# First mixer: sums of squares against two columns of ones in place of 128

## The chip, the cores and the metric

The kernel runs on one core of a Trainium2 chip. The metric is the device time of one execution in microseconds (us); lower is better. The core has a matrix engine (TensorE, PE in the rows; its weight loads are listed apart as PEld), VectorE (DVE), ScalarE (ACT), GpSimd (POOL), and a queue that starts DMA transfers (SP). They run side by side and wait for each other by semaphores.

## The reference, cut to what matters

Two blocks of two layers each are computed for 256 tokens of width 1024, in float32. A layer of the first block is a mixer and then a mixture of experts. At its end the mixer normalises two halves of 512 features (attention heads, short convolution) apart and multiplies with `w_out`:

```python
def rmsnorm(x, g):
    y = x * lax.rsqrt(jnp.mean(x * x, axis=-1, keepdims=True) + EPS)
    return y * g

y_attn = windowed_gqa_with_sink(q, k, v, sink)            # (tokens, 512)
y_conv = gate_b * centred_short_conv(gate_c * u, conv_w)  # (tokens, 512)
y = jnp.concatenate([rmsnorm(y_attn, g_attn), rmsnorm(y_conv, g_conv)], axis=-1)
x = x + y @ w_out
```

So each token needs two sums of squares, each over 512 features: 4 numbers for each of 128 partitions, as the 256 tokens are two tiles of 128. The experts, the final norm and the whole second block follow and are not touched.

## The kernel before, in words

The kernel is one program of five instruction streams in an order written out by hand. `psum_tiles()` numbers every PSUM tile; tile n lies in bank n mod 8 and a semaphore for each bank counts fillings (`done`, `full`) and emptyings (`claim`, `emptied`). An engine executes its stream strictly as written, TensorE's included; its weight loads can run ahead of the matmuls in front of them.

In the first mixer everything before the norm is held with the features on the partitions: `yT` (the two halves, scaled by their gains) and `sq` (their squares, written by ScalarE at lines 812 and 831), each 8 blocks of 128 features by 256 tokens. A sum over features is a sum over partitions, which TensorE does: at line 1901, after the heads' loop, it takes a 128 by 128 block of `sq` (128 features, 128 tokens) as the stationary operand and the constant `ones` as the moving operand. The result has the tokens on the partitions, and every column of it holds the same sum. Four blocks of features are accumulated for each of the 2 halves and the 2 token tiles, so line 1901 has 16 matmuls in a layer. Each float32 matmul runs as two load-and-multiply pairs, so the trace shows 32 matmuls and 32 loads a layer, 64 of each in all. All four results lie in one PSUM bank, tile `("ss", layer, 0)`.

What reads it is one VectorE instruction at line 1249, which takes one column of each of the four results, and makes mean plus EPS. GpSimd raises that to the power -1/2 (line 683, `inverse_root`). VectorE then adds the products with `w_out` to `x`, scaled by these roots (line 1258, 8 times). The products are the tiles `out1`: `mixer_out(i)` at line 1858 makes each with 4 matmuls of 512 columns. Two of them (`out1` 0 and 1) stand ahead of the sums of squares on TensorE, beside the last heads, and six behind; after the fifth of those come transposes of `x` (line 1912), the router (line 1923, matmuls of 36 columns) and `keep_clock` (line 1739), matmuls of zeros with `ones` that have no result anyone reads.

In the expert stage (lines 1779 to 2063) line 2035 multiplies 128 by 128 blocks with a moving operand of 2 columns, 128 times in all.

Of the kernel before, what the change touches and what calls it, by code (L numbers as in the profile page):

```python
# [23 lines left out]
P = 128  # L24
# [166 lines left out]
def program(nc, x_in, cols_in, rows_in, rope1_in, gains_in, router_in, w_in, w_out, w_gate, w_up, w_down,  # L191
            positions, w_in2, w_lru, w_oa, w_or, w_o, out):
    with ExitStack() as ctx:
# [12 lines left out]
        ones = ctx.enter_context(nc.sbuf_tensor("ones", [P, P], F32))  # L206
# [15 lines left out]
        stat = ctx.enter_context(nc.sbuf_tensor("stat", [P, 64], F32))  # L222
# [11 lines left out]
        def carve(phase, *shape):  # L234
            n = int(np.prod(shape))
            at = top.get(phase, 0)
            top[phase] = at + n
            assert top[phase] <= WORK, (phase, top[phase])
            v = work[:, at:at + n]
            if len(shape) == 2:  # L240
                v = v.rearrange("p (a b) -> p a b", a=shape[0])
            if len(shape) == 3:
                v = v.rearrange("p (a b c) -> p a b c", a=shape[0], b=shape[1])
            return v
# [19 lines left out]
        sq = carve("mix1", KD, SEQ)  # L264
# [155 lines left out]
        def bank(name):  # L420
            return banks[TILE[name] % BANKS]
# [5 lines left out]
        def uses(name):  # L427
            return TILE[name] // BANKS + 1

        def full(eng, name):  # L430

            eng.wait_ge(psum_full[TILE[name] % BANKS], uses(name))
# [51 lines left out]
        def arrive2(eng, layer, j):  # L484

            at = layer * NB2 + j
            kind, _, n = B2_PIECES[j]
            eng.wait_ge(w_loaded["b2"][at % RING2], 16 * (at // RING2 + 1))
            if kind == "lru":
                return ring[:, at % RING2, 0:n].rearrange("p (b n) -> p b n", n=P)  # L490
            return piece(at % RING2, RT if kind == "or" else KD, n)
# [581 lines left out]
        def _(dve):  # L1073
            S = Steps(dve, own_dve)
# [92 lines left out]
            def first_mixer(layer):  # L1167
# [13 lines left out]
                for t in range(NT):  # L1181
                    a, b = heads[t][:, :, 0:ROT1], heads[t][:, :, ROT1:2 * ROT1]
# [5 lines left out]
                for t in range(NT):  # L1188
                    a, b = heads[t][:, :, 0:ROT1], heads[t][:, :, ROT1:2 * ROT1]
# [49 lines left out]
                for hh in range(HEADS):  # L1239
# [3 lines left out]
                    for nm, j in BESIDE_HEAD[hh]:  # L1243
                        if nm == "u":
                            gated_input(j)

                name = ("ss", layer, 0)
                full(dve, name)
                S.marks(dve.tensor_scalar(stat[:, 8:12], bank(name)[:].rearrange("p (a b) -> p a b", b=P)[:, :, 0],
                                          1.0 / CW, EPS, ALU.mult, ALU.add), psum_read[TILE[name] % BANKS], uses(name))  # L1250
                dve.wait_ge(rstd_ready, 5 * layer + 3)
                for i in range(8):
                    hf, t, part = OUT1[i]
                    name = ("out1", layer, i)
# [458 lines left out]
            for layer in range(DEPTH):  # L1713
                first_mixer(layer)
                last_hT(2 * layer + 1)
                router(layer)
                experts(layer)
# [7 lines left out]
        def _(pe):  # L1725
# [59 lines left out]
            for layer in range(DEPTH):  # L1785
# [12 lines left out]
                else:  # L1798
# [5 lines left out]
                    for k0 in (0, KD // 2):  # L1804
# [4 lines left out]
                        for t in range(NT):  # L1809
                            for k in range(k0, k0 + KD // 2):  # L1810
                                mm = pe.matmul(bank(("q", 0, t))[:], hT[:, k, t * P:(t + 1) * P], w[:, k],
                                               start=(k == 0), stop=(k == KD - 1))
# [16 lines left out]
                for j in range(3):  # L1829
                    name = ("qkT", layer, j)  # L1830
                    claim(name)
                    for k in range(2):
                        for t in range(NT):
                            src = (qkv[:, t, (2 * j + k) * P:(2 * j + k + 1) * P] if j < 2 else
                                   (qkv[:, t, QW:QW + KVW] if k == 0 else kswap[:, t]))
                            mm = pe.transpose(bank(name)[:, k * SEQ + t * P:k * SEQ + (t + 1) * P], src, ident[:])
# [27 lines left out]
                for hh in range(HEADS):  # L1864
                    if hh + 1 < HEADS:
                        scores(hh + 1)
                    name = ("PT1", layer, hh)
                    claim(name)
                    pe.wait_ge(probs, layer * HEADS + hh + 1)
                    for kb in range(NT):  # L1870
                        for qb in range(NT):
                            mm = pe.transpose(bank(name)[:, kb * SEQ + qb * P:kb * SEQ + (qb + 1) * P],
                                              s1[:, hh % 2, qb, kb * P:(kb + 1) * P], ident[:])
# [13 lines left out]
                    for kb in range(NT):  # L1887
                        mm = pe.matmul(bank(yn)[r, 0:SEQ], qkv[:, kb, v0:v0 + HD1], pT1[:, hh % 2, kb],
                                       start=(kb == 0), stop=(kb == NT - 1))
# [5 lines left out]
                name = ("ss", layer, 0)  # L1895
                claim(name)
                for part in range(2):
                    for t in range(NT):
                        o = (2 * part + t) * P
                        for j in range(4):  # L1900
                            mm = pe.matmul(bank(name)[:, o:o + P], sq[:, 4 * part + j, t * P:(t + 1) * P], ones[:],
                                           start=(j == 0), stop=(j == 3))
                done(mm, name)
                def turn_x(t):
# [31 lines left out]
                name = ("rank", layer, 0)  # L1936
# [7 lines left out]
                mm = pe.matmul(bank(name)[:, 2 * NE:3 * NE], ones[:], A[:, 1], start=False, stop=True)  # L1944
# [115 lines left out]
                for t in range(NT):  # L2060
                    for hf in range(2):
                        for part in (y_hi, y_lo):
                            mm = pe.matmul(banks[2 * t + hf][:], comb[:, 1, t * P:(t + 1) * P],
                                           part[:, hf * 512:(hf + 1) * 512], start=False, stop=True,
                                           skip_group_check=True)
# [3 lines left out]
            for layer in range(DEPTH):  # L2069
# [120 lines left out]
                for j in range(0, 12, 2):  # L2190
# [4 lines left out]
                    for k in range(cnt):  # L2195
                        for odd in range(2):
                            if j < 4:
                                hd, qb = 8 * (j // 2) + 2 * k + odd, 0
                            else:
                                hd, qb = 4 * ((j - 4) // 2) + 2 * k + odd, 1  # L2200
                            r = slice(64 * odd, 64 * odd + 64)
                            mm = pe.matmul(bank(names[odd])[:, k * w_:(k + 1) * w_], iqT[r, hd // 2, qb * P:(qb + 1) * P],
                                           ikT[r, 0:w_], start=True, stop=True)
# [8 lines left out]
                for j in range(RT):  # L2212
                    name = ("gates", layer, j)
                    claim(name)
                    mine = [(n, i) for n, (jj, i) in enumerate(BLOCK_PAIRS) if jj == j]
                    for g, wg_ in enumerate((wr, wi)):
                        for n, i in mine:
                            mm = pe.matmul(bank(name)[:, g * SEQ:(g + 1) * SEQ], wg_[:, n], xc[:, i],  # L2218
                                           start=(n == mine[0][0]), stop=(n == mine[-1][0]))
# [22 lines left out]
                for hh in range(HEADS):  # L2242
                    if hh + 1 < HEADS:
                        scores2(hh + 1)
                    name = ("PT2", layer, hh)
                    claim(name)
                    pe.wait_ge(probs2, layer * HEADS + hh + 1)
                    b = hh % 2
# [80 lines left out]
```

## Time and profile before

| | us |
|---|---|
| median of 3 runs | 1988.59 |
| lowest, highest | 1988.37, 1990.35 |
| profiled execution, its own time | 1990.61 |
| profiled execution, its span (first to last instruction) | 1988.9 |
| TensorE busy with matmuls | 1909.9 (96% of the span) |
| TensorE busy with weight loads | 1272.3 (64%) |
| VectorE busy | 734.3 (37%) |
| mean granted clock of TensorE | 0.992 of full speed |

A row of the trace gives the start in us from the span's start, the duration, the engine, the line of the kernel, the operation, what it writes and reads (`work` holds `sq`), the shape, and the number of instructions that were merged into the row. In brackets stands how long the engine was idle before and who ended that. The end of a matmul is modelled. "Granted clock" is the share of TensorE's full speed that the chip allowed; 1.00 is 2.4 GHz and 0.50 is 1.2 GHz.

### The profile page before, as it was taken

The numbers are of one execution on the slowest core, as the hardware profiler recorded it, in microseconds if no ns is written. First come the engines' busy times: TensorE is split into PE (matmuls) and PEld (weight loads), VectorE is DVE, ScalarE is ACT, GpSimd is POOL, SyncE is SP. The second block draws the span as 40 slices with busy tenths as digits, with TensorE's granted clock in tenths as the row PEclk, the third lists the DMA queues.
The fourth block names the chain that finished last, engine by engine and source line by source line (L and its number), as shares of the span: only waits on it lengthen the run. The fifth ranks groups of instructions, "written<-read, shape, count | busy, mean of one in ns | idle before, by whom it ended". The sixth has DMA issues, their size and how long they took to land.

```text
span 1988.9 us, 26083 instructions
## 1 busy us (share of the span) xinstructions
PE 1909.9 (96%) x10488; PEld 1272.3 (64%) x10488; DVE 734.3 (37%) x1679; ACT 606.5 (30%) x1170; POOL 266.5 (13%) x247
## 2 busy tenths in 40 slices
PE   8999999999998999999999999999999989999997
PEld 6764444444445754444444445887889968788996
DVE  3332111111112332111111114556665645656655
ACT  2311111111112321111111113556654534574654
POOL 1300000000000300000000003971000057710000
PEclk9999999999999999999999999999999999999999
DMA  9348999999998238999999996452425845433353
GB/s 363 113 169 363 427 428 427 428 429 428 428 417 302 87 147 366 428 427 427 428 428 428 429 428 231 138 199 85 167 81 160 287 143 170 167 122 110 111 177 118
DMA packets 121421, 557.47 MB, mean 280 GB/s; under 512 B 5008, under 2 KB 49584, under 8 KB 96240
## 3 DMA queue, kind: packets, MB, share of 16 engines
q1 hardware_dynamic: 119696, 551.51, 69.9%
q10 hardware_dynamic: 1440, 4.36, 0.6%
q8 instruction: 65, 1.06, 0.2%
q0 software_dynamic: 192, 0.30, 0.1%
q14 instruction: 28, 0.23, 0.0%
HBM read 555.11 MB, written 1.05 MB: 280 GB/s over the span
## 4 chain that ended last, share of the span: by engine, by line
PE 90%; ACT 4%; DVE 4%; issue 2%; POOL 0%; POOLq 0%; DVEq 0%
PE bank L2015 15%; PE bank L2046 11%; PE bank L2017 8%; PE bank L1771 7%; PE bank L1779 6%; PE bank L2160 3%; PE bank L2162 3%; PE bank L2161 3%; PE bank L1992 3%; PE bank L2139 3%; PE bank L2140 3%; PE bank L2141 3%; PE bank L1763 3%; PE bank L1858 3%; PE bank L2218 3%
## 5 line engine op out<-in xcount | busy, mean ns | idle before, releaser
L2015 PE MATMUL bank<-ring,work 128*64 128x512 f32 x512 | 224.9, 594 | 5.0 <-issue 5.0
L2017 PE MATMUL bank<-ring,work 128*64 128x512 f32 x512 | 224.9, 594 | 0.0
L727 POOL TENSOR_TENSOR w_lo<-ring,w_hi 128x512 fp32r<-128x512 f32 (+1 forms) x160 | 207.7, 1319 | 78.0 <-ACT w_hi L917 75.6
L683 POOL TENSOR_TENSOR stat<-stat,power 128x1 f32<-128x1 f32 (+1 forms) x18 | 10.8, 601 | 1502.2 <-DVE stat L1079 1465.4
L1421 DVE TENSOR_TENSOR work<-work,bank 64x512 f32<-64x512 f32 x64 | 43.9, 686 | 433.3 <-ACT work L872 433.3
L872 ACT ACTIVATE work<-bank 64x512 f32<-64x512 f32 x64 | 37.8, 591 | 474.3 <-PE bank L2017 474.3
L917 ACT CAST w_hi<-ring 128x512 fp32r<-128x512 f32 (+1 forms) x208 | 123.3, 606 | 131.4 <-PE bank L2162 87.7
L1640 DVE TENSOR_TENSOR w_lo<-ring,w_hi 128x512 fp32r<-128x512 f32 (+1 forms) x176 | 116.0, 678 | 79.3 <-ACT w_hi L1030 79.1
L1771 PE MATMUL bank<-hT,ring 128*128 128x256 f32 x640 | 143.6, 379 | 0.0
L1779 PEld LDWEIGHTS bank<-work,h 128*128 128x128 f32 x1024 | 116.7, 192 | 24.8 <-issue 24.8
L1030 ACT CAST w_hi<-ring 128x512 fp32r<-128x512 f32 (+1 forms) x176 | 104.0, 610 | 92.9 <-PE bank L2141 76.4
L1771 PEld LDWEIGHTS bank<-hT,ring 128*128 128x128 f32 x640 | 119.4, 190 | 15.7 <-issue 0.7
L1437 DVE SCALAR_TENSOR_TENSOR act_hi<-bank,stat,act_hi 128x512 fp32r<-128x512 f32 x64 | 48.1, 751 | 211.1 <-ACT act_hi L882 211.1
L2015 PEld LDWEIGHTS bank<-ring,work 128*64 128x64 f32 x512 | 68.5, 137 | 88.6 <-issue 86.6
L1779 PE MATMUL bank<-work,h 128*128 128x128 f32 x1024 | 122.8, 278 | 0.1
L2015 PE MATMUL bank<-ring_tail,work 128*64 128x512 f32 x256 | 113.0, 594 | 3.2 <-issue 3.2
L2046 PE MATMUL bank<-ring,work 128*64 128x512 f32 x512 | 113.4, 595 | 2.2 <-ACT work L877 0.8
L2015 PE MATMUL bank<-work 128*64 128x512 f32 x256 | 112.9, 594 | 2.5 <-issue 2.5
L2017 PE MATMUL bank<-ring_tail,work 128*64 128x512 f32 x256 | 113.1, 595 | 0.0
L2017 PE MATMUL bank<-work 128*64 128x512 f32 x256 | 113.0, 594 | 0.0
L882 ACT ACTIVATE act_hi<-bank,stat 128x512 fp32r<-128x512 f32 x64 | 44.0, 687 | 210.4 <-PE bank L2046 210.4
L753 ACT ACTIVATE work<-bank 128x256 f32<-128x256 f32 (+3 forms) x128 | 57.9, 476 | 154.9 <-PE bank L1771 61.1
(317 smaller groups left out, 3829.5 us busy)
## 6 DMA issues: line engine op xcount, KB each, us to landing
ring<-w_in_dram SPq DMA_DIRECT2D x34, 2048.0 KB, 9.1
ring<-w_gate_dram SPq DMA_DIRECT2D x32, 2048.0 KB, 18.5
ring<-w_up_dram SPq DMA_DIRECT2D x32, 2048.0 KB, 23.0
ring<-w_down_dram SPq DMA_DIRECT2D x32, 2048.0 KB, 23.2
ring_tail<-w_down_dram SPq DMA_DIRECT2D x16, 2048.0 KB, 21.0
work<-w_gate_dram SPq DMA_DIRECT2D x16, 2048.0 KB, 18.5
work<-w_up_dram SPq DMA_DIRECT2D x16, 2048.0 KB, 22.9
ring_tail<-w_gate_dram SPq DMA_DIRECT2D x16, 2048.0 KB, 19.9
```

The source lines that it names most:

```text
L727: pool.tensor_tensor(w_lo[:, g % CHUNKS, 0:n], w[:, k], w_hi[:, g % CHUNKS, 0:n], ALU.subtract).then_inc(chunk_lo, 1)
L917: act.copy(w_hi[:, g % CHUNKS, 0:w.shape[2]], w[:, k]).then_inc(chunk_hi, 1)
L1030: act.copy(w_hi[:, g % CHUNKS, 0:src.shape[1]], src).then_inc(chunk_hi, 1)
L1640: dve.tensor_tensor(w_lo[:, g % CHUNKS, 0:n], src, w_hi[:, g % CHUNKS, 0:n], ALU.subtract).then_inc(chunk_lo, 1)
L1763: mm = pe.matmul(bank(name)[:, 0:n], hT[:, k, t * P:(t + 1) * P], w[:, k, 0:n], start=(k == 0), stop=(k == KD - 1))
L1771: mm = pe.matmul(dst, w[:, k, f * P:(f + 1) * P], rhs[:, k], start=(k == 0), stop=(k == nk - 1))
L1779: mm = pe.matmul(dst[:, kk * P:(kk + 1) * P], h[:, t, k * P:(k + 1) * P], pick[:, b, t], start=(t == 0), stop=(t == NT - 1))
L1858: mm = pe.matmul(bank(name)[:], yT[:, 4 * part + j, t * P:(t + 1) * P], w_[:, 4 * part + j], start=(j == 0), stop=(j == 3))
L1992: mm = pe.matmul(banks[2 * t + hf][:], comb[:, p % 2, t * P:(t + 1) * P], part[:, hf * 512:(hf + 1) * 512], start=(first and p == 0 and pa ...
L2015: pe.matmul(m_bank(m)[gate, :], lhs, wg[:, k], start=(k == 0), stop=(k == KD - 1), skip_group_check=True)
L2017: mu = pe.matmul(m_bank(m)[up, :], lhs, wu[:, k], start=(k == 0), stop=(k == KD - 1), skip_group_check=True)
L2046: mm = pe.matmul(m_bank(m0 + T_OUT + hf)[r, :], hidT[:, f * P + 64 * side:f * P + 64 * side + 64], wd[side][:, f, hf * 512:(hf + 1) * 512] ...
```

## The change

The moving operand at line 1901 becomes the first 2 columns of `ones`, and the four results stand side by side in the first 8 columns of the bank. The reader at line 1249 takes every second column of these 8. The number of matmuls and of weight loads, the stationary operands, the PSUM tile, all semaphores and the order on every engine stay.

```diff
-                S.marks(dve.tensor_scalar(stat[:, 8:12], bank(name)[:].rearrange("p (a b) -> p a b", b=P)[:, :, 0],
+                S.marks(dve.tensor_scalar(stat[:, 8:12], bank(name)[:, 0:8].rearrange("p (a b) -> p a b", b=2)[:, :, 0],
                                           1.0 / CW, EPS, ALU.mult, ALU.add), psum_read[TILE[name] % BANKS], uses(name))
...
                 for part in range(2):
                     for t in range(NT):
-                        o = (2 * part + t) * P
+                        o = 2 * (2 * part + t)
                         for j in range(4):
-                            mm = pe.matmul(bank(name)[:, o:o + P], sq[:, 4 * part + j, t * P:(t + 1) * P], ones[:],
+                            mm = pe.matmul(bank(name)[:, o:o + 2], sq[:, 4 * part + j, t * P:(t + 1) * P], ones[:, 0:2],
                                            start=(j == 0), stop=(j == 3))
```

On TensorE, at the end of the first layer's mixer, the difference of the two programs reads (a row is one kind of instruction in a line of the kernel, with its count; the second layer has the same):

```order
 L1858 MATMUL bank<-ring_tail,work 128x512 x4
 L1888 MATMUL bank<-work 64x256 x2
-L1901 MATMUL bank<-ones,work 128x128 x16
+L1901 MATMUL bank<-ones,work 128x2 x16
 L1858 MATMUL bank<-ring_tail,work 128x512 x20
 L1912 MATMUL bank<-ident,x 128x128 x8
```

Nothing is moved; one row has another width. On the four other engines the rows are the same in both programs.

## Rows read from the trace of the kernel before

**Rows 1.** The page: busy time, then the chain that ended last, by engine.
```profile
PE 1909.9 (96%) x10488; PEld 1272.3 (64%) x10488; DVE 734.3 (37%) x1679; ACT 606.5 (30%) x1170; POOL 266.5 (13%) x247
...
PE 90%; ACT 4%; DVE 4%; issue 2%; POOL 0%; POOLq 0%; DVEq 0%
```

**Rows 2.** The chain in order of time, 107.8 to 114.2 us: start, duration, what.
```profile
107.89 1.02 PE bank L1888 x4
108.92 0.02 issue
108.94 0.38 ACT work L831
109.32 0.37 ACT work L753
109.70 0.25 issue
109.94 3.81 PE bank L1901 x32
113.75 0.86 PE bank L1858 x2
```

**Rows 3.** The timeline of 105 to 122 us, first layer.
```profile
109.91 3.65 PEld L1901 LDWEIGHTS bank<-ones,work 128*128 128x128 f32 x32 [1.47 <-issue]
109.94 3.81 PE L1901 MATMUL bank<-ones,work 128*128 128x128 f32 x32 [1.04 <-ACT work L753]
113.48 0.30 PEld L1858 LDWEIGHTS bank<-ring_tail,work 128*128 128x128 f32 x2
113.59 8.75 PE L1858 MATMUL bank<-ring_tail,work 128*128 128x512 f32 x20
113.79 0.17 DVE L1249 TENSOR_SCALAR stat<-bank 128x4 f32<-128x4 f32 x1 [11.98 <-PE bank L1901]
114.03 1.05 POOL L683 TENSOR_TENSOR stat<-stat,power 128x4 f32<-128x4 f32 x1 [17.56 <-DVE stat L1249]
...
115.12 1.62 DVE L1258 SCALAR_TENSOR_TENSOR x<-bank,stat,x 128x512 f32<-128x512 f32 x2 [1.16 <-POOL stat L683]
...
117.23 0.75 DVE L1258 SCALAR_TENSOR_TENSOR x<-bank,stat,x 128x512 f32<-128x512 f32 x1 [0.49 <-PE bank L1858]
```

**Rows 4.** Line 1901 alone, both layers: durations as ns min/median/max.
```profile
L1901 PEld LDWEIGHTS bank<-ones,work x64: 186/192/192, 109.9 to 714.8; 128*128 128x128 f32 x64
L1901 PE MATMUL bank<-ones,work x64: 275/275/348, 109.9 to 715.0; 128*128 128x128 f32 x64
```

**Rows 5.** Timelines of other narrow stretches: line 2035, line 1923, line 1739.
```profile
168.23 0.53 PEld L2035 LDWEIGHTS bank<-work 128*128 128x128 f32 x4
...
168.34 0.51 PE L2035 MATMUL bank<-work 128*128 128x2 f32 x4
...
135.40 0.75 PEld L1923 LDWEIGHTS bank<-work,hT 128*128 128x128 f32 x6
...
140.47 4.99 PEld L1739 LDWEIGHTS bank<-ones,zeros 128*128 128x128 f32 x44
```

**Rows 6.** Line 2035 alone: durations as ns min/median/max.
```profile
L2035 PEld LDWEIGHTS bank<-work x128: 190/192/192, 168.2 to 1196.8; 128*128 128x128 f32 x128
L2035 PE MATMUL bank<-work x128: 170/251/251, 168.3 to 1196.8; 128*128 128x2 f32 x128
```

**Rows 7.** The chain again: line 1858 in both layers, line 1901 in the second.
```profile
99.16 3.70 PE bank L1858 x8
...
698.94 5.40 PE bank L1858 x8
...
711.42 3.81 PE bank L1901 x32
```

**Rows 8.** Stretches: length, busy us of each engine, granted clock, DMA share, GB/s.
```profile
95.00:105.00 10.00, 8.74 (x32) 4.33 (x31) 2.83 (x9) 5.97 (x18) 0.72 (x1) 1.00 0.57 210
695.00:705.00 10.00, 8.74 (x25) 3.99 (x24) 2.61 (x8) 5.47 (x17) 0.72 (x1) 0.83 0.58 211
109.94:113.75 3.81, 3.81 (x33) 3.81 (x34) 0.00 (x0) 0.00 (x0) 0.00 (x0) 1.00 0.00 0
113.75:130.92 17.17, 17.17 (x43) 7.55 (x42) 5.37 (x9) 1.15 (x2) 1.58 (x2) 1.00 0.33 123
1348.00:1352.00 4.00, 1.22 (x10) 0.76 (x8) 3.47 (x10) 1.76 (x4) 0.00 (x0) 0.91 0.16 57
1352.00:1356.00 4.00, 3.65 (x9) 2.90 (x10) 3.48 (x8) 1.00 (x2) 0.00 (x0) 0.50 0.02 4
1356.00:1360.00 4.00, 4.00 (x15) 3.19 (x14) 3.65 (x7) 1.21 (x2) 2.59 (x2) 0.74 0.00 0
```

## The prediction

> **What bounds the kernel now.** I read the page first, then the chain of waits around the edit, the timeline of the same stretch, and then looked for places where the kernel already does what the change does. The page says that TensorE is busy 96% of the span and makes 90% of the chain that ended last [rows 1]. So a microsecond taken from TensorE can be a microsecond gained, if TensorE has nothing else to wait for. The chain shows that this holds at the edit: TensorE ends the last head's product at 108.91, waits 1.04 us for ScalarE to write the last squares, runs line 1901 for 3.81 us, and goes on at 113.75 with the products of line 1858 [rows 2]. That stretch lasts 17.17 us, with TensorE busy in all of it [rows 8]. The second layer shows the same 3.81 us [rows 7].
>
> The whole question is therefore what sets the pace within these 3.81 us. The timeline lists two streams of 32 there: matmuls over 3.81 us and weight loads over 3.65 us [rows 3]. A load takes 192 ns [rows 4], the first one starts the stretch and the last ends it, so the loads follow each other every (3.65 - 0.19) / 31 = 0.1116 us. The matmuls cannot be closer than the loads, since each has its own block of squares. What the reader must see is that the two streams have one pace, and that the row alone does not say which of them sets it.
>
> **The width.** The stream's own price comes from line 1858: 20 instructions of 512 columns take 8.75 us [rows 3], 0.44 us each or 0.85 ns a column, the last one's tail included. So 128 columns cost at most 0.11 us and 2 columns 0.002 us. Before the change load and stream are thus nearly equal, 0.11 us each, side by side. Taking the stream away leaves the load, if a load of 128 columns really needs the 0.11 us by itself.
>
> That is what the trace has a direct answer for. Line 2035 has the form that line 1901 will have: a 128 by 128 float32 block against 2 columns, accumulated. Its 4 loads take 0.53 us [rows 5], so they follow each other every (0.53 - 0.19) / 3 = 0.113 us. The router's loads with 36 moving columns follow every (0.75 - 0.19) / 5 = 0.112 us, and those of line 1739, with 128 columns, every (4.99 - 0.19) / 43 = 0.112 us [rows 5]. Widths of 2, 36 and 128 columns give one pace; it is the load's. The saving at line 1901 is 32 x (0.1116 - 0.112), which is zero within the rounding. Nothing can be gained from the 32 loads, since the change keeps all of them.
>
> In the other direction, eight instructions now accumulate on the same two columns one right behind the other. Line 2035 does that with four and keeps 0.113 us, so I add nothing.
>
> At this place the Trainium skill has two rules that disagree with each other, in "TensorE: Matmul & The Clock Gate". Its section "Back-to-back issue gap" gives a lone matmul N/2.4 + 2.5 ns and a floor of about 25 ns for few columns, 31 ns less for each of the 64 instructions, an estimate of 2.0 us saved in all. Its section "LDWEIGHTS (loading the stationary operand)" gives P/1.2, 107 ns for 128 columns whatever moves, an estimate of nothing saved. By the second the trace agrees, with 0.113 us at 2 columns [rows 5]; the first is the stream's bound alone.
>
> **The ends of the stretch.** At the front nothing changes: the wait of 1.04 us is for ScalarE. At the back, the first load of line 1858 starts at 113.48 and its first matmul at 113.59, one load later [rows 3]. That matmul waits for its load, not for the end of the 128 columns before it, so it starts where it did: gain 0, at most the 0.1 us by which the last stream is shorter, 0.2 us for both layers.
>
> **The reader.** The last matmul of the sums is listed with 275 ns before [rows 4] and would be with 251 ns after, as at line 2035 [rows 6]. So VectorE's line 1249 starts about 0.02 us earlier, then GpSimd's root, then the first two additions to `x`. There the gain ends: VectorE next waits 0.49 us for TensorE's product [rows 3]. The same 0.49 us is the cover if the reader should come later; a read of columns 2 apart in place of 128 apart is still 4 elements on a partition, and would have to cost four times its 0.17 us to be seen. DMA and SP are not touched in the stretch: the DMA share there is 0.00 [rows 8].
>
> **The sum.** Loads 0, stream 0 (covered by the loads), tail 0 to -0.2 us, reader 0 (covered by the wait for TensorE). I take -0.05 us for both layers, nearer to the zero of the load-bound rows. Against the profiled execution that is 1990.61 - 0.05 = 1990.56, with a span of 1988.85 and the same 1.7 us around it. The profiled execution lay 2.0 us above the median of the runs, so the median after comes to 1988.59 - 0.05, or 1988.5. A measurement of this kernel can tell from no change what is over about 0.2%, 4.0 us.
>
> **Rival one, slower: the granted clock falls behind the sums.** What the change does take away is work in the array: in 3.6 us TensorE would multiply 2 columns for each load where it had 128, and 1.04 us of waiting lie ahead of it. The trace shows that this chip lowers the clock to 1.2 GHz while TensorE is far from idle. In the second layer, between 695 and 705, TensorE is busy for 8.74 of 10 us and the granted clock of the stretch is 0.83, against 1.00 for the same work in the first layer [rows 8]; 8 instructions of line 1858 took 5.40 us there in place of 3.70 [rows 7]. So one place can go either way. One such drop costs 5.40 - 3.70 = 1.7 us. A longer one lies at 1348 to 1360, with clocks 0.91, 0.50 and 0.74 over 4 us each [rows 8]: 6.8 us at 1.2 GHz, half of it lost, 3.4 us. The point from which it decides is whether the clock is kept through 1.04 us of waiting and 3.6 us in which TensorE loads weights and multiplies almost nothing. As what follows is 17 us of unbroken TensorE work, all of the loss goes to the end. Price: 3.4 us with one short drop in each layer, 1992.0; 6.8 us with a long one in each, 1995.4; 1.7 us with a drop in only one layer, 1990.2. For it: the drop between 695 and 705 came with TensorE busy for most of the time. Against it: after the sums with 128 columns the clock was 1.00 [rows 8], and the 2-column matmuls of line 2035 last only 0.5 us, so no row shows a long stretch of that kind, for or against.
>
> The Trainium skill's "TensorE: Matmul & The Clock Gate" says, under "What's actually happening", that a monitor sets the gate by how busy the PE has been recently. It does not say whether a weight load counts as busy. If it does, the rule leaves the time as it is; if it does not, it gives this rival's 3.4 us or more.
>
> **Rival two, faster: the pace is the stream's in part.** At line 2035 the 4 matmuls span 0.51 us, (0.51 - 0.25) / 3 = 0.087 us apart, less than the loads' 0.113 [rows 5]. If a long row kept that pace, 64 x (0.112 - 0.087) = 1.6 us would go, 1987.0. Against it: only the first pair there is close, as its loads were done while wider transposes streamed; 32 in a row use up such a lead at once.
>
> **Rival three: a stall between writes to the same two columns.** From the nearest rows it is 0.001 us for each instruction (0.113 against 0.112), 0.1 us in all; if each cost as much as another load, 64 x 0.11 = 7 us, 1995.6. Line 2035 speaks against it.
>
> **How the numbers follow.** The forecast, no difference, gets 0.60 (its own range 1987.0 to 1990.4, which is the spread of the runs shown around it). Rival one gets 0.34: 0.22 for a loss of up to 4 us, 0.12 beyond. Rival two gets 0.04, of which 0.02 for a gain over 0.2%, if the cause were larger than I can see. Rival three gets 0.02. Within 0.2%: 0.60 + 0.22 + 0.02 + 0.01 = 0.85; slower 0.13; faster 0.02. The range runs from 1986.9, below rival two, to 1992.4, which takes in the short drops of rival one and leaves out its long ones.
>
> **What would show it.** In the changed profile line 1901 should have 32 loads in 3.65 us again, its matmuls about 251 ns each instead of 275, and line 1858 should start 3.6 us after line 1901 does. VectorE's line 1249 should still be 0.17 us. A granted clock below 1.00 between 110 and 120 or between 711 and 722, and line 1858 stretched there, would mean rival one, and the prediction would be wrong by 1.7 us for each such drop. Loads closer than 0.11 us would mean rival two.

## The result, and the profile after

The changed kernel is slower: 1997.61 us median of 8 runs (1995.28 to 2001.80) against 1990.62 for the kernel before (8 runs, 1988.14 to 1993.40), ratio 1.0034, 95% interval 1.0025 to 1.0043. Run again in a later series the ratio was 1.0024 (1.0014 to 1.0033). The forecast was 1988.5 with a range up to 1992.4; the result lies outside the range. Of the 9.1 us between forecast and result, 2.0 belong to the kernel before, whose first three executions had a median of 1988.59 and all eight 1990.62. The change made 7.0.

The page of the profiled execution (own time 1998.18, span 1996.4) looks like the one of [rows 1] but for its span, 7.5 us more:

```profile
span 1996.4 us, 26083 instructions
PE 1915.6 (96%) x10488; PEld 1276.6 (64%) x10488; DVE 733.6 (37%) x1679; ACT 606.4 (30%) x1170; POOL 266.6 (13%) x247
```

The chain at the edit, first layer, answers to [rows 2]; its last two rows are those of the second layer:

```profile
108.15 1.02 PE bank L1888 x4
...
109.58 0.37 ACT work L753
109.95 0.25 issue
110.20 4.63 PE bank L1901 x32
114.82 19.70 PE bank L1858 x40
...
715.19 5.39 PE bank L1901 x32
720.58 18.91 PE bank L1858 x40
```

Line 1901 takes 4.63 and 5.39 us where it took 3.81, and the 40 instructions of line 1858 behind it take 19.70 and 18.91 us where they took 17.17. The first layer thus loses 0.82 + 2.53 = 3.35 us, the second 1.58 + 1.74 = 3.32.

The same line alone, to be laid beside [rows 4] (ns min/median/max):

```profile
L1901 PEld LDWEIGHTS bank<-ones,work x64: 186/192/338, 110.2 to 720.2; 128*128 128x128 f32 x64
L1901 PE MATMUL bank<-ones,work x64: 243/251/354, 110.2 to 720.2; 128*128 128x2 f32 x64
```

The medians are as forecast: 192 ns for a load, 251 for a matmul of 2 columns. The longest load is new, 338 ns in place of 192. Something slows part of the stretch. What it is stands in the stretches' rows (length, busy us of each engine, granted clock, DMA share, GB/s), to be laid beside [rows 8]:

```profile
105.00:110.00 5.00, 4.16 (x12) 1.59 (x10) 0.00 (x0) 1.09 (x3) 0.00 (x0) 1.00 0.00 0
110.00:115.00 5.00, 4.80 (x33) 4.83 (x34) 0.14 (x1) 0.00 (x0) 0.00 (x0) 0.78 0.00 0
115.00:120.00 5.00, 5.00 (x7) 2.04 (x7) 1.52 (x3) 0.00 (x0) 1.05 (x1) 0.54 0.00 0
120.00:125.00 5.00, 5.00 (x13) 2.17 (x12) 1.49 (x2) 0.00 (x0) 0.00 (x0) 1.00 0.01 3
...
715.19:720.58 5.39, 5.39 (x33) 5.39 (x33) 0.00 (x0) 0.00 (x0) 0.00 (x0) 0.66 0.00 0
```

The same view in steps of 0.5 us gives the place of the fall in each layer:

```profile
112.00:112.50 0.50, 0.50 (x7) 0.50 (x6) 0.00 (x0) 0.00 (x0) 0.00 (x0) 1.00 0.00 0
112.50:113.00 0.50, 0.50 (x6) 0.50 (x5) 0.00 (x0) 0.00 (x0) 0.00 (x0) 0.75 0.00 0
113.00:113.50 0.50, 0.50 (x4) 0.50 (x4) 0.00 (x0) 0.00 (x0) 0.00 (x0) 0.50 0.00 0
...
716.50:717.00 0.50, 0.50 (x6) 0.50 (x6) 0.00 (x0) 0.00 (x0) 0.00 (x0) 0.91 0.00 0
```

The granted clock is 1.00 up to 110, 0.78 and 0.54 in the next two stretches of 5 us, and 1.00 again. If TensorE ran at 1.2 GHz for a share s of a stretch and at 2.4 GHz for the rest, the mean is 1 - s/2, so the time at 1.2 GHz is 2 x (0.22 + 0.46) x 5 = 6.8 us. TensorE was busy for nearly all of it, and half of it is lost, 3.4 us. In this execution the clock fell at about 112.8 and 716.9, some 2.6 and 1.7 us after line 1901 began, and not in the wait ahead of it.

The loss is not given back. The experts (line 1779) start at these times before and after, in the chain:

```profile
148.45 3.81 PE bank L1779 x32
...
749.94 3.81 PE bank L1779 x32
```
```profile
152.06 3.81 PE bank L1779 x32
...
757.01 3.81 PE bank L1779 x32
```

That is 3.61 us late in the first layer (0.26 of it was there ahead of the sums, as line 1888 started at 108.15 and not 107.89) and 7.07 in the second; at the end it is 7.5. The drop of the clock shortly before the second layer's sums is in both profiles (5.40 us for the 8 instructions of line 1858, [rows 7], and again 5.40 after), so it does not explain the difference.

The reader behaved as forecast:

```profile
114.86 0.16 DVE L1249 TENSOR_SCALAR stat<-bank 128x4 f32<-128x4 f32 x1 [12.80 <-PE bank L1901]
...
120.83 0.75 DVE L1258 SCALAR_TENSOR_TENSOR x<-bank,stat,x 128x512 f32<-128x512 f32 x1 [3.03 <-PE bank L1858]
```

Reading columns 2 apart takes 0.16 us where columns 128 apart took 0.17, and VectorE now waits 3.03 us for TensorE's product in place of 0.49.

### The profile page after: what moved, and what is told of

It reads as the page before. It is cut to its first block, busy times and chain, and to the rows that moved or that the text cites. A ratio compares the mean times of both kernels' runs of the same rounds, so it can differ in the third digit from the quotient of the medians.

```text
span 1996.4 us, 26083 instructions
## 1 busy us (share of the span) xinstructions
PE 1915.6 (96%) x10488; PEld 1276.6 (64%) x10488; DVE 733.6 (37%) x1679; ACT 606.4 (30%) x1170; POOL 266.6 (13%) x247
## 4 chain that ended last, share of the span: by engine, by line
PE 90%; ACT 4%; DVE 4%; issue 2%; POOL 0%; POOLq 0%; DVEq 0%
PE bank L2015 15%; PE bank L2046 11%; PE bank L2017 8%; PE bank L1771 7%; PE bank L1779 6%; PE bank L2160 3%; PE bank L2162 3%; PE bank L2161 3%; PE bank L1992 3%; PE bank L1858 3%; PE bank L2139 3%; PE bank L2140 3%; PE bank L2141 3%; PE bank L1763 3%; PE bank L2218 3%
```

## The experiments

The theory (A): the chip lowers TensorE's clock because line 1901, with the wait ahead of it, has become a stretch in which next to nothing is multiplied. The rivals: the loss lies elsewhere (B); the narrow matmuls or their place in the bank cost by themselves (D, E); only waits matter, and any matmul keeps the clock (C). Times below are medians; each ratio is to the kernel before in the same series. The code differences are shortened, with `...` or a comment where something is left out, and each is against the kernel that its minus lines show.

### One layer at a time

```diff
-  mm = pe.matmul(bank(name)[:, o:o + P], sq[...], ones[:], ...)
+  n = 2 if layer == 1 else P          # e9: layer == 0
+  mm = pe.matmul(bank(name)[:, o:o + n], sq[...], ones[:, 0:n], ...)
```

> Two columns in the second layer only, 128 in the first. Theory A (the granted clock falls behind each layer's sums, 3.4 us lost for each): half of the loss, about 3.4 us over the kernel before; the first layer's line 1901 takes 3.81 us again with a clock of 1.00 between 110 and 130, and the second layer's takes over 3.81 us with a long stretch at 1.2 GHz. Theory B (the loss comes from elsewhere, such as other places where the clock falls in one execution and not in another): the whole 7 us or nothing, and no tie to the layer.

> Two columns in the first layer only. The second layer alone (e1) lost 3.4 us between its last head and its experts in the profiled execution, but only 1 us in the medians. Theory A: the first layer does the same, a stretch at 1.2 GHz between 110 and 130, 3.4 us lost there, and the medians show 2 to 5 us. If the clock falls only in a part of the executions in either layer, the times of single executions lie in groups some 1.7 us apart, and the median is 1 to 3.4 us over before.

Second layer only (e1): 1993.42 against 1992.41, ratio 1.0003 (0.9993 to 1.0013), single executions from 1990.97 to 1997.97. First layer only (e9): 1995.19 against 1992.23, ratio 1.0018 (1.0009 to 1.0027). The stretches from 105 to 135 and from 708 to 738, first of e1 and then of e9:

```profile
105.00:135.00 30.00, 28.96 (x103) 15.28 (x101) 7.85 (x11) 2.97 (x6) 1.59 (x2) 1.00 0.19 70
708.00:738.00 30.00, 28.96 (x94) 15.71 (x93) 7.80 (x11) 2.97 (x6) 1.58 (x2) 0.89 0.19 70
```
```profile
105.00:135.00 30.00, 28.96 (x92) 16.06 (x91) 6.86 (x9) 2.91 (x6) 1.58 (x2) 0.89 0.19 70
708.00:738.00 30.00, 28.96 (x104) 15.37 (x103) 7.98 (x11) 2.97 (x6) 1.58 (x2) 1.00 0.19 70
```

Of the two places the clock falls only where the two columns are: 0.89 over 30 us is 2 x 0.11 x 30 = 6.6 us at 1.2 GHz, 3.3 us lost. So B does not hold for the loss seen in the profiles. The first layer's 3 us by the medians fit the 3.4. The second layer's 1 us does not: e1 expected 3.4 and its interval ends at 2.6. Its profiled execution did lose 3.3 us there. Its ten executions have mean granted clocks from 0.988 to 0.993, so they did not all lose the same; in how many of them the clock fell at this place stays open. Nor is the rest of the program still: from 1580 to 1620 us the clock is 0.96 in the profiled execution of the kernel before and 0.87 in those of e1 and e9, 3.2 and 10.4 us at 1.2 GHz. Drops elsewhere come and go too, and move a time by some microseconds.

### The width

```diff
-  o = 2 * (2 * part + t)
+  o = 64 * (2 * part + t)             # e3: 32
-  mm = pe.matmul(bank(name)[:, o:o + 2], sq[...], ones[:, 0:2], ...)
+  mm = pe.matmul(bank(name)[:, o:o + 64], sq[...], ones[:, 0:64], ...)
```

> 64 columns in both layers, four blocks of 64 side by side. Theory A: the array multiplies for about half of the stretch, the clock stays at 1.00 behind the sums or falls less often; time within 2 us of before. If the loss hangs on the layout or on fewer columns as such, the time is the changed kernel's, 7 us over before. In either case 32 loads at 0.112 us each while the clock is full.

> 32 columns in both layers. Theory A, if less and less in the array is what counts: between the kernels with 128 and with 2 columns, 0 to 7 us over before, with the clock below 1.00 behind the sums in some executions. Theory C (a matmul of any width keeps the clock, only the waits count): no difference from 128 columns, which the changed kernel already speaks against.

With 64 columns 1994.13, ratio 1.0010 (1.0001 to 1.0020); with 32 columns 1997.50, ratio 1.0026 (1.0016 to 1.0035), both against 1992.41. In the profiled execution with 64 columns the clock stayed at 1.00 behind the first layer's sums and was 0.89 over 30 us behind the second's; with 32 it was 0.89 behind both. So in the profiled executions one layer of two lost the clock with 64 columns and both did with 32, as with 2. C has fallen: behind the same wait, 128 columns kept the clock and 32 did not.

### The layout in the bank

```diff
-  mm = pe.matmul(bank(name)[:, o:o + P], sq[...], ones[:], ...)
+  mm = pe.matmul(bank(name)[:, o:o + 2], sq[...], ones[:, 0:2], ...)   # o stays 128 apart
```

> Two columns, but with the four results 128 columns apart, so that the reader at line 1249 is the one of before. Theory A: the clock falls behind the sums as in the changed kernel, line 1901 takes more than 3.81 us and line 1858 is stretched, time 1995 to 2001. Theory D (it is the eight columns side by side, in one small place of the bank): line 1901 takes 3.81 us or less, the clock stays, time as before.

A single execution: 1997.46. Line 1249 took 162 ns, as in the changed kernel:

```profile
L1249 DVE TENSOR_SCALAR stat<-bank x2: 161/162/163, 114.9 to 717.5; 128x4 f32<-128x4 f32 x2
```

and the clock was 0.83 from 105 to 135 and 0.94 from 708 to 738, 10.2 and 3.6 us at 1.2 GHz. The clock falls without the eight columns side by side, so D is not needed; one execution does not tell whether the layout changes how long it stays low.

### The same narrow matmuls between wide ones

```diff
-  # 16 sums in a row, then out1 2, out1 3, ...
+  for n in range(8):                               # the 8 matmuls of out1 2 and 3
+      mm = pe.matmul(bank(name)[:], yT[...], w_[...], ...)
+      for part, t, j in terms[2 * n:2 * n + 2]:
+          mm = pe.matmul(bank(ss)[:, o:o + 2], sq[...], ones[:, 0:2], ...)
```

> Two columns, with two of the 16 sums behind each of the 8 matmuls of out1 2 and 3 (512 columns each). The same matmuls, the same loads and columns in all. Theory A: the wide matmuls lie in between, the clock stays at 1.00, and the time is that of the kernel before within 1 us (the loads of the sums are not hidden: only one can run ahead). Theory E (each narrow matmul costs by itself): as slow as the changed kernel, 7 us.

1991.53 against 1991.23, ratio 1.0006 (0.9998 to 1.0015). The clock was 1.00 in both stretches. The chain shows 8 times a pair like this, the products (line 1904 there) and the sums (line 1910):

```profile
110.44 0.96 PE bank L1904 x2
111.40 0.34 PE bank L1910 x4
```

With wide matmuls between them the two columns showed no cost (the interval ends at 3 us), and E, which asked for 7, has fallen. They also gain nothing: a pair of instructions of 512 columns takes 0.96 us in place of 0.86, and the four narrow ones 0.34, together 0.44 us for 4 loads, 0.11 us each again. Here, too, the loads are not hidden beneath the wide streams.

### The wait ahead of the sums filled, with 2 and with 128 columns

```diff
+  mixer_out(4)                        # the convolution half's product, ready long before
   for j in range(4):
       emptied(pe, ("Y1", layer, j))
...
-  for i in range(2, 7):
+  for i in (2, 3, 5, 6):
       mixer_out(i)
```

> Two columns, and the product out1 4, which needs only the convolution half, moved ahead of the sums, where TensorE waited 1.04 us for ScalarE. The wait goes (about 1.3 us with the issue behind it in each layer, 2.5 us in all). Theory A with the wait as a needed part of the quiet stretch: the clock falls less often, time 1988 to 1993. Theory A with the sums alone enough: the clock falls in both layers as in the changed kernel, time about 2.5 us below it, 1995.

> The same move with 128 columns as before the change. The clock stays at 1.00 behind the sums; TensorE's wait of 1.04 us and the 0.25 us behind it are filled in each layer: about 2.5 us below the kernel before, 1988. If something else is late in place of the wait (the products' weights, a bank), the gain is under 1 us.

With 2 columns 1993.14 (1988.24 to 1998.89), with 128 columns 1988.37 (1987.59 to 1990.31), both against 1991.23: ratios 1.0008 (0.9998 to 1.0018) and 0.9985 (0.9977 to 0.9994). With 128 columns the move brings the kernel before 2.9 us, near the 2.5 expected. With 2 columns it does not beat the kernel before, though it is nearer to it (1.0008) than the changed kernel is (1.0024 and 1.0034). Its clock was 0.94 over 30 us in both layers, 3.6 us at 1.2 GHz in each, half of what the changed kernel had. The wait was a part of the quiet stretch, and the sums alone are enough to lose the clock in the profiled execution.

These two runs also compare the widths with no wait ahead. The sums with 2 columns (first line, e5), which had the full clock until the last 0.3 us, take as long as those with 128 (second line, e6):

```profile
112.64 3.57 PE bank L1902 x32
```
```profile
111.38 3.57 PE bank L1902 x32
```

### A shorter stretch, and idleness in place of the loads

```diff
-  for j in range(4):
+  for j in range(1):                  # e8 and e10
...
+  for again in range(9 if j == 3 else 1):          # e10, on ScalarE
+      if again: S.settle()
       S(act.activation(sq[:, j], bank(("Y1", layer, j))[:, 0:SEQ], ACT.Square))
```

> Two columns, and only one of the four blocks of features is summed (the other three are left out): 8 loads and matmuls a layer in place of 32, 2.7 us of TensorE's time less in each layer. Theory A: the quiet stretch is 1.04 + 0.9 us, the clock stays or falls rarely, time 5.4 us below before, 1985. If the few columns or the place and not the length of the stretch were the cause: clock lost in both layers again, 7 us more than that.

> As e8 (one of the four blocks summed, two columns), but ScalarE writes the last squares nine times over, so that TensorE waits some 3 us longer ahead of line 1901: the quiet stretch has about the length of the changed kernel's, with idleness in place of 24 weight loads. Theory A with weight loads counting for nothing: the same stretches at 1.2 GHz as in the changed kernel, about 6.8 us in each layer, time 1995 to 2000. If the weight loads had kept the clock in part: more or longer stretches here than in the changed kernel, and over 2000.

Both kernels leave out three of the four blocks of features, so their output is not the reference's.

e8: 1987.50 against 1991.23, ratio 0.9982 (0.9973 to 0.9991). Against the kernel before it has 5.4 us of loads less, and 3.7 came back. Its profile shows the rest: clock 0.94 over 30 us in the first layer, 1.8 us lost, and 1.00 in the second. So 1.04 us of waiting with 1.02 us of narrow matmuls was followed by a drop in one layer of two.

e10: 1996.95 against 1992.23, ratio 1.0036 (1.0022 to 1.0049). Its timeline in the first layer, and then its stretches:

```profile
107.78 1.08 PE L1891 MATMUL bank<-work 128*64 128x256 f32 x4
113.22 1.84 PE L1904 MATMUL bank<-ones,work 128*128 128x2 f32 x8 [4.37 <-ACT work L753]
114.92 10.39 PE L1861 MATMUL bank<-ring_tail,work 128*128 128x512 f32 x19
```
```profile
105.00:135.00 30.00, 25.63 (x67) 12.40 (x66) 6.04 (x9) 5.22 (x14) 1.59 (x2) 0.89 0.19 70
708.00:738.00 30.00, 25.63 (x63) 12.09 (x62) 5.01 (x9) 5.57 (x13) 1.58 (x2) 0.89 0.19 70
```

TensorE was idle for 4.37 us and then made 8 loads, where the changed kernel was idle for 1.04 and made 32. The clock came out the same, 0.89 over 30 us in both layers, though here it fell at about 112.1, before the first of the 8 loads:

```profile
112.00:112.50 0.50, 0.00 (x0) 0.00 (x0) 0.00 (x0) 0.47 (x2) 0.00 (x0) 0.62 0.00 0
```

So in these executions a stream of weight loads that multiply two columns kept the clock no better than idleness did; whether the loads count for something is not shown beyond that. The times agree: a layer has 3.33 us more idleness and 24 loads of 0.112 us less than the changed kernel, 0.6 us more, or 1.3 in all, and e10 came out 1.2 us above the changed kernel in the same series (1996.95 against 1995.71). The expectation of more than 2000 for the other reading was not met by the median; one of the five executions was over it.

### A version that beats both

```diff
+  # VectorE, with the move of e6 and 128 columns
+  dve.wait_ge(conv_sq, 4 * layer + 4)
+  S(dve.tensor_tensor(sq[:, 4:6], sq[:, 4:6], sq[:, 6:8], ALU.add))
+  S(dve.tensor_tensor(sq[:, 0], sq[:, 0], sq[:, 1], ALU.add))
+  S.settle()
+  S(dve.tensor_tensor(sq[:, 4], sq[:, 4], sq[:, 5], ALU.add))
+  S(dve.tensor_tensor(sq[:, 0], sq[:, 0], sq[:, 2], ALU.add), sq_sum)
...
-  for j in range(4):                  # blocks 4 * part + j
+  for j in ((0, 3), (4,))[part]:      # TensorE: 6 matmuls in place of 16
```

> 128 columns, out1 4 ahead as in e6, and VectorE, which is idle there, adds up the blocks of squares that are ready (four of the convolution half into one, three of the heads' four into one), so that TensorE has 6 matmuls for the sums in place of 16: 20 weight loads at 0.112 us less in each layer, 2.2 us. Expected 4.5 us below e6, 1984, with the clock at 1.00 behind the sums. If the sums' result is not what TensorE waits for and VectorE's five additions come late, TensorE waits for them and the gain is under 2 us.

1984.60 (1981.72 to 1986.68, 5 runs) against 1992.23, ratio 0.9965 (0.9951 to 0.9978). The chain in the first layer (line 1911 is the sums):

```profile
108.10 3.63 PE bank L1865 x8
111.73 1.34 PE bank L1911 x12
113.07 8.16 PE bank L1865 x19
```

12 instructions take 1.34 us in place of 32 in 3.81, no wait stands ahead of them, and the clock was 1.00 in both layers' stretches. By the ratios it lies 4.0 us below e6, where 4.5 were expected. This takes away loads, which are what line 1901 costs.

### The changed kernel once more

> The changed kernel once more, on the chip of the three others. Theory A: 6 to 8 us over before, in both layers a stretch below full clock from line 1901 into line 1858, and more scatter between executions than the kernel before has.

1995.71 (1994.47 to 2000.95) against 1992.23 (1988.81 to 1994.39), 3.5 us by the medians and 1.0024 (1.0014 to 1.0033) by the ratio; the 6 to 8 us expected were too many for this series. Its profiled execution, at 2000.95, had clocks of 0.89 and 0.83 over the two stretches of 30 us, 6.6 and 10.2 us at 1.2 GHz. The size of the loss thus differs from one execution to the next, and so do the medians of two series.

The profiles show one execution of each kernel. The mean granted clock was taken in every execution; here are the averages over a run's executions and over those of the kernel before in the same series:

| run | what it has | clock | before |
|---|---|---|---|
| e12 | 2 columns, the changed kernel | 0.9899 | 0.9918 |
| e3 | 32 columns | 0.9892 | 0.9918 |
| e10 | 2 columns, 8 loads, longer wait | 0.9892 | 0.9918 |
| e2 | 64 columns | 0.9908 | 0.9918 |
| e1 | 2 columns, second layer only | 0.9907 | 0.9918 |
| e9 | 2 columns, first layer only | 0.9905 | 0.9918 |
| e5 | 2 columns, no wait | 0.9909 | 0.9921 |
| e7 | 2 columns between wide matmuls | 0.9920 | 0.9921 |
| e6 | 128 columns, no wait | 0.9927 | 0.9921 |

For the changed kernel the difference of 0.0019 over 1992 us is 3.8 us of full clock, and its median is 3.5 us over before. So the clock accounts for the loss over all executions of this series and not only in the profiled one. In the first series the changed kernel's eight executions average 0.9894; the clocks of the kernel before are on record there for the profiled execution alone (0.992).

## Why the prediction was wrong, point by point

- **The loads set the pace: right.** At full clock they follow each other as before, which e7 shows apart from the clock (0.11 us each). Median durations were 192 and 251 ns as forecast, and 32 instructions took 3.57 us with 2 columns (e5) as with 128 (e6). Nothing was gained by the width.
- **No stall on the same two columns, no cost of the reader: right.** In e5 eight instructions in a row went to the same two columns and kept the pace; the reader took 0.16 us.
- **The clock: the step that failed.** The sum had terms for loads, stream, tail and reader and none for the clock: it took "the loads are unchanged" for "the time is unchanged", and the fall of the clock stood beside it as a rival with a chance of 0.34. What the runs showed is rival one, with its mechanism, its place (behind the wait and within the sums) and its long price, 3.4 us in each layer, 6.8 in all; measured 7.0 by the medians and 7.5 by the spans of the first series, but 3.5 by the medians of the second. That the first series comes so near to 6.8 is in part chance. The point on which that rival was said to hang is answered by e10: the clock is not kept through such loads.
- **The weighing.** The rows for it were in hand, but the prediction read them over too long a stretch. The 8.74 of 10 us [rows 8] take in the work behind the fall. Cut where the clock fell, the same trace reads:

```profile
695.07:698.94 3.87, 2.61 (x12) 1.44 (x12) 1.61 (x3) 3.87 (x12) 0.72 (x1) 1.00 0.74 226
698.94:702.35 3.41, 3.41 (x5) 1.46 (x6) 0.94 (x4) 1.60 (x6) 0.00 (x0) 0.56 0.85 360
```

Ahead of the fall TensorE was busy for 2.61 of 3.87 us, with matmuls of 128 and 256 columns, and idle for the last 1.26: a wait hardly longer than the 1.04 us at line 1901 was followed by a drop in the second layer and by none in the first. Rival one was priced with one short drop in each layer as its main case; the long one had its price from the stretch at 1348 to 1360 and was left outside the range. In the changed kernel's profiled execution the clock fell within the sums (0.78 over 110 to 115), while the quiet went on, and the rest of the loads ran at 1.2 GHz. That the quiet itself grows when the clock falls in it, 3.81 to 4.63 and 5.39 us, was not in the estimate.
- The Trainium skill's "TensorE: Matmul & The Clock Gate", under "What's actually happening", lets the gate follow how busy the PE has been. e10 agrees if weight loads count little or not at all as being busy: with 24 of them replaced by idleness the clock was 0.89 over 30 us in both layers, as with them.

## What to carry to other kernels

Here a narrower moving operand saved nothing, since every matmul has a stationary block of its own and the loads set the pace at 2 as at 128 columns. It can cost: 3.6 us in which TensorE did little but load weights were, for its clock, like waiting. Look at the granted clock of the stretch, not at the busy share, before taking columns out of it, and place narrow matmuls between wide ones (e7) or take away their loads by adding up operands on an engine that is idle (e11). A row at 128 columns that seems wasteful may be what holds the clock.

## What the runs showed of the hardware

- A run of 32 loads with 2-column matmuls, behind 1.04 us of waiting, brought 6.8 us at 1.2 GHz in each layer of the changed kernel, and 3.6 to 10.2 in e4 and e12; a run with 32 columns brought 6.6. With 64 columns one layer of two kept 1.00 in the profiled execution, with 128 both.
- 4.37 us of idleness and 8 such loads gave the same clock as 1.04 us and 32, 0.89 over 30 us.
- A float32 load of a 128 by 128 block with its matmul takes 0.112 us at full clock, with 2 columns as with 128: 32 in 3.57 us in e5 and in e6.
- With 2 columns the executions also lay farther apart: 1988.24 to 1998.89 in the 12 of e5, against 1987.59 to 1990.31 in the 11 of e6, the same kernel with 128.
